# Second layer's heads: exponentials read from the banks by ScalarE, two scalings moved to ScalarE, the mask ahead of the exponential, background pieces moved behind

## The reference, cut to what matters

```python
dmat = jnp.where(order, b[..., :, None] - b[..., None, :] + ig[..., None, :], -jnp.inf)
m_t = jnp.maximum(inter, jnp.max(dmat, axis=-1))
s = jnp.einsum('bhtd,bhsd->bhts', q, k) * jnp.exp(dmat - m_t[..., None])
...
h = num / jnp.maximum(jnp.abs(den), jnp.exp(-m_t))[..., None]
...
h = (h_f + flip(h_b)) if emit else None
...
y = jax.nn.sigmoid(o.astype(f32)).reshape(B, T, M_HEADS, M_DV) * h
y = _rmsnorm(y, hn.reshape(M_HEADS, M_DV)).reshape(B, T, M_V).astype(z.dtype)
return (y * jax.nn.silu(z)) @ w_out
```

## Time and profile before

| | |
|---|---|
| median of three runs | 2987.8 us (2987.46 to 2990.23) |
| profiled execution, its own time | 2990.57 us |
| its span in the profile | 2988.8 us |
| granted TensorE clock, share of full speed | 0.996 |
| busy: PE, DVE, ACT, POOL | 98%, 70%, 39%, 3% of the span |
| heads of the second layer | from about 593 to 1327 us, some 101 us a head |

### The profile page before, as it was taken

One profiled execution on the slowest core, in us unless ns is written; L12 is line 12 of the kernel. 1 busy time (PEld: TensorE's weight loads), 2 busy tenths in 40 slices (PEclk: granted clock), 3 DMA queues, 4 the chain that ended last, 5 costly groups with the idle time before them and its releaser, 6 DMA issues.

```text
span 2988.8 us, 43582 instructions
## 1 busy us (share of the span) xinstructions
PE 2932.5 (98%) x17098; PEld 2353.5 (79%) x17098; DVE 2090.1 (70%) x3957; ACT 1178.0 (39%) x2056; POOL 103.5 (3%) x188
## 2 busy tenths in 40 slices
PE   8999999999999999999999999999999999999999
PEld 7777778888888888878888888888888888885346
DVE  4576876788888776677666886677675678765455
ACT  4322323322332232242245555455444445543344
POOL 0000000000000000000000000000010120000000
PEclk9999999999999999999999999999999999999999
DMA  9777784354555455538636774645576443487997
GB/s 366 281 266 286 273 282 149 127 169 148 190 168 177 162 183 169 179 128 275 235 117 206 258 241 142 197 148 180 195 236 218 141 164 128 152 274 259 403 404 314
DMA packets 193197, 641.69 MB, mean 215 GB/s; under 512 B 21488, under 2 KB 36192, under 8 KB 192992
## 3 DMA queue, kind: packets, MB, share of 16 engines
q1 hardware_dynamic: 132080, 423.44, 40.6%
q10 hardware_dynamic: 58032, 207.12, 20.3%
q0 software_dynamic: 2880, 8.35, 0.9%
HBM read 624.15 MB, written 12.58 MB: 213 GB/s over the span
## 4 chain that ended last, share of the span: by engine, by line
PE 87%; DVE 7%; ACT 3%; DMA 2%; issue 1%; SPq 0%; DVEq 0%; ACTq 0%; POOL 0%; POOLq 0%
PE PS L506 15%; PE PS L502 11%; PE PS L504 9%; PE PS L505 9%; PE PS L635 7%; PE PS L637 7%; PE PS L636 7%; PE PS L1061 2%; PE PS L798 2%; PE PS L1472 2%; DMA AR<-e_w 1%; DVE WL L2389 1%; PE PS L1441 1%; PE PS L1428 1%; PE PS L1122 1%
## 5 line engine op out<-in xcount | busy, mean ns | idle before, releaser
L2389 DVE TENSOR_TENSOR WL<-WR,WH 128x1024 fp32r<-128x1024 f32 (+1 forms) x566 | 682.4, 1211 | 401.7 <-ACT WH L1574 400.5
L506 PE MATMUL PS<-HT,WL 128*128 128x256 f32 (+1 forms) x2928 | 951.5, 325 | 0.0
L1574 ACT ACTIVATE WH<-WR 128x1024 fp32r<-128x1024 f32 (+1 forms) x566 | 587.1, 1044 | 873.1 <-PE PS L506 486.7
L506 PEld LDWEIGHTS PS<-HT,WL 128*128 128x128 f32 x2928 | 552.1, 189 | 47.6
L502 PE MATMUL PS<-HT,WH 128*128 128x512 f32 x1584 | 566.0, 401 | 9.2 <-DVE WL L2389 6.1
L504 PE MATMUL PS<-HT,WH 128*128 128x512 f32 (+1 forms) x1344 | 518.4, 386 | 5.4 <-DVE HT L2369 2.4
L505 PE MATMUL PS<-HT,WH 128*128 128x512 f32 (+1 forms) x1344 | 507.9, 378 | 0.0
L635 PE MATMUL PS<-WH,HT 128*128 128x512 f32 x1016 | 402.7, 396 | 3.5 <-DVE HT L2369 2.5
L637 PE MATMUL PS<-WH,HT 128*128 128x512 f32 x1016 | 396.8, 391 | 0.0
L636 PE MATMUL PS<-WL,HT 128*128 128x512 f32 x1016 | 396.2, 390 | 0.0
L502 PEld LDWEIGHTS PS<-HT,WH 128*128 128x128 f32 x1584 | 297.4, 188 | 90.2 <-issue 13.1
(11 more groups left out here) (472 smaller groups left out, 3319.1 us busy)
## 6 DMA issues: line engine op xcount, KB each, us to landing
WR<-ada_w SPq DMA_DIRECT2D x264, 512.0 KB, 4.6
AR<-e_w SPq DMA_DIRECT2D x88, 512.0 KB, 10.0
E_RING<-e_w SPq DMA_DIRECT2D x80, 512.0 KB, 10.2
WR<-m_vo ACTq DMA_DIRECT2D x64, 512.0 KB, 4.6
WR<-a_qz ACTq DMA_DIRECT2D x64, 512.0 KB, 4.8
WR<-n_m SPq DMA_DIRECT2D x64, 512.0 KB, 4.3
AR<-ada_p ACTq DMA_DIRECT2D x56, 512.0 KB, 6.3
AR<-ada_p SPq DMA_DIRECT2D x48, 512.0 KB, 8.0
```

Of the source, the lines that this page charges most:

```text
L506: return e.matmul(ps[:, 0:b - a], wl, HH_[:, c, a:b], start=False, stop=c == last)
L1574: e.activation(part_of(WH, s), place_of(plan["slot"][p])[:, 0:width(s)], ACT.Copy, scale=1.0).then_inc(*L.up(hi_done, ("hi", s)))
L2389: e.tensor_tensor(part_of(WL, s), place_of(plan["slot"][plan["split"][s]])[:, 0:width(s)], part_of(WH, s).bitcast(F32), ALU.subtract).then ...
```

## The change

Per head:

- VectorE's `ts` (add and clamp) is gone. ScalarE adds the column term itself from the bank, as the bias of the activation: for the diagonal 128x128 blocks with Identity (8 instructions, `pt`), for the whole blocks of `M_REST` straight with Exp (7 instructions). GpSimd masks the diagonal blocks before the exponential, with -3e38, and ScalarE takes their exponential last (8 instructions).
- VectorE multiplies by S only where there is a weight (`M_BLOCKS`): 9 instructions in place of 8, 2560 columns in place of 3072.
- The scaling of the d = 0 results into `M_HH` is done by ScalarE (4 Copy instructions, event `pvx`), and so is the scaling by the inverse root (4, `yn`). VectorE's reciprocals have names now (`pvs`, `yi`) on which ScalarE waits.
- `bg(2)` behind k goes; in `along_vo` the calls at q = 2 and q = 5 take two pieces in place of one, for heads 1 to 7.

```diff
--- before.py
+++ after.py
+    M_BLOCKS = {(0, 0): [(0, 512)], (0, 1): [(0, 128), (256, 512)], (1, 0): [(128, 512)], (1, 1): [(0, 512)],
+                (2, 0): [(256, 512)], (2, 1): [(256, 384)], (3, 0): [(384, 512)], (3, 1): [(256, 512)]}
+    M_REST = {(0, 0): [(128, 512)], (0, 1): [(256, 512)], (1, 0): [(256, 512)], (1, 1): [(0, 128), (256, 512)],
+              (2, 0): [(384, 512)], (2, 1): [], (3, 0): [], (3, 1): [(256, 384)]}
...
@@ scalar_program, mlstm
+            w.wait_ge(L.at("columns"))
             for h in range(8):
+                if h:
+                    w.wait_ge(L.at(("p_used", h - 1)))
+                for d in range(2):
+                    ps, free = place[("cb", h, d)], ("free", ("cb", h, d))
+                    w.wait_ge(L.at(("full", ("cb", h, d))))
+                    for k in range(4):
+                        t = slice(128 * k, 128 * k + 128)
+                        e.activation(M_P[d][:, m_at(k, t.start, t.stop)], ps[:, t], ACT.Identity,
+                                     bias=M_ACOL[:, k, 32 * d + h:32 * d + h + 1], scale=1.0).then_inc(
+                            *L.up(act_done, ("pt", h, k, d), free))
+                    for k in range(4):
+                        for a, b in M_REST[k, d]:
+                            e.activation(M_P[d][:, m_at(k, a, b)], ps[:, a:b], ACT.Exp,
+                                         bias=M_ACOL[:, k, 32 * d + h:32 * d + h + 1], scale=1.0).then_inc(
+                                *L.up(act_done, ("pe", h, k, d), free))
                 for k in range(4):
-                    n = 512 if k < 2 else 256
                     for d in range(2):
-                        p = M_P[d][:, M_PC[k]:M_PC[k] + n]
-                        w.wait_ge(L.at(("pt", h, k, d)))
+                        p = M_P[d][:, m_at(k, 128 * k, 128 * k + 128)]
+                        w.wait_ge(L.at(("pa", h, k, d)))
                         e.activation(p, p, ACT.Exp, scale=1.0).then_inc(*L.up(act_done, ("pe", h, k, d)))
...
+                if h:
+                    w.wait_ge(L.at(("hh_used", h - 1)))
+                for tb in range(4):
+                    w.wait_ge(L.at(("pvs", h, tb, 0)))
+                    e.activation(M_HH[:, tb, :], place[("pv", h, tb, 0)][:, 0:256], ACT.Copy,
+                                 scale=M_ST[2 * tb % 4][:, 0:1]).then_inc(
+                        *L.up(act_done, ("pvx", h, tb), ("free", ("pv", h, tb, 0))))
...
+                w.wait_ge(L.at(("yi", h)))
+                for tb in range(4):
+                    e.activation(M_HH[:, tb, :], M_HH[:, tb, :], ACT.Copy, scale=s[:, 8 + tb:9 + tb]).then_inc(
+                        *L.up(act_done, ("yn", h, tb)))
                 if h < 7:
                     vo(h + 1)
...
@@ vector_program, mlstm
                 for q in range(first, 8):
                     cut_to(plan[("vo", h)][0] + q + NP)
-                    bg(1)
+                    bg(2 if q in (2, 5) and h else 1)
...
             for h in range(8):
-                w.wait_ge(L.at(*(("full", ("cb", h, d)) for d in range(2))))
-                if h:
-                    w.wait_ge(L.at(("p_used", h - 1)))
                 for k in range(4):
                     c0 = 0 if k < 2 else 256
                     for d in range(2):
-                        p = M_P[d][:, M_PC[k]:M_PC[k] + 512 - c0]
-                        ts(p, place[("cb", h, d)][:, c0:512], M_ACOL[:, k, 32 * d + h:32 * d + h + 1], 0.0,
-                           ALU.add, ALU.min, ("pt", h, k, d), *([("free", ("cb", h, d))] if k == 3 else []))
...
-                        w.wait_ge(L.at(("pa", h, k, d), ("full", ("S", h, k))))
-                        tt(p, p, place[("S", h, k)][:, 0:512 - c0], ALU.mult, ("p", h, k, d), ("free", ("S", h, k)))
+                        w.wait_ge(L.at(("pe", h, k, d), ("full", ("S", h, k))))
+                        for a, b in M_BLOCKS[k, d]:
+                            p = M_P[d][:, m_at(k, a, b)]
+                            tt(p, p, place[("S", h, k)][:, a - c0:b - c0], ALU.mult, ("p", h, k, d), ("free", ("S", h, k)))
...
                     elif k == 3 and h < 7:
                         along(("k", h + 1))
-                        bg(2)
...
-                        recip(s, s)
-                        w.wait_ge(L.last(dve_done))
-                        if d == 0:
-                            scaled(M_HH[:, tb, :], ps[:, 0:256], s, ALU.mult, ("free", ("pv", h, tb, d)))
-                        else:
+                        recip(s, s, ("pvs", h, tb, d))
+                        if d:
+                            w.wait_ge(L.last(dve_done), L.at(("pvx", h, tb)))
                             stt(M_HH[:, tb, :], ps[:, 0:256], s, M_HH[:, tb, :], ALU.mult, ALU.add,
...
-                recip(s[:, 8:12], s[:, 8:12])
-                w.wait_ge(L.last(dve_done))
-                for tb in range(4):
-                    scaled(M_HH[:, tb, :], M_HH[:, tb, :], s[:, 8 + tb:9 + tb], ALU.mult, ("yn", h, tb))
+                recip(s[:, 8:12], s[:, 8:12], ("yi", h))
...
@@ gpsimd_program, mlstm
-                        w.wait_ge(L.at(("pe", h, k, d)))
-                        e.affine_select(out=pd, in_=pd, compare_op=ALU.is_ge, fill=0.0, base=0,
+                        w.wait_ge(L.at(("pt", h, k, d)))
+                        e.affine_select(out=pd, in_=pd, compare_op=ALU.is_ge, fill=-3e38, base=0,
```

More of the change, by code:

```diff
@@ L198, in _program, with m_at @@
     M_PC = [0, 512, 1024, 1280]
+    M_BLOCKS = {(0, 0): [(0, 512)], (0, 1): [(0, 128), (256, 512)], (1, 0): [(128, 512)], (1, 1): [(0, 512)],
+                (2, 0): [(256, 512)], (2, 1): [(256, 384)], (3, 0): [(384, 512)], (3, 1): [(256, 512)]}
+    M_REST = {(0, 0): [(128, 512)], (0, 1): [(256, 512)], (1, 0): [(256, 512)], (1, 1): [(0, 128), (256, 512)],
+              (2, 0): [(384, 512)], (2, 1): [], (3, 0): [], (3, 1): [(256, 384)]}
+    def m_at(k, a, b):
+        at = M_PC[k] - (0 if k < 2 else 256)
+        return slice(at + a, at + b)
     M_KEYS = {0: ([0], [0, 1]), 1: ([0, 1], [1]), 2: ([0, 1, 2], [0, 1, 2, 3]), 3: ([0, 1, 2, 3], [0, 1, 3])}
@@ L2911, in mlstm @@
             w.wait_ge(L.at(("full", ("gt",))))
-            copy(SML[:, 0:320], place[("gt",)][:, 0:320], ("free", ("gt",)))
+            copy(SML[:, 0:320], place[("gt",)][:, 0:320], "columns", ("free", ("gt",)))
             w.wait_ge(L.last(dve_done))
             for h in range(8):
-                w.wait_ge(L.at(*(("full", ("cb", h, d)) for d in range(2))))
-                if h:
-                    w.wait_ge(L.at(("p_used", h - 1)))
                 for k in range(4):
@@ L2938, in mlstm @@
                         along(("k", h + 1))
-                        bg(2)
-                if h:
-                    w.wait_ge(L.at(("hh_used", h - 1)))
                 for tb in range(4):
@@ L2945, in mlstm @@
                         s = M_ST[(2 * tb + d) % 4][:, 0:1]
-                        den = ps[:, 256:257]
                         w.wait_ge(L.at(("full", ("pv", h, tb, d))))
-                        stt(s, den, -1.0, M_ECOL[:, tb, 32 * d + h:32 * d + h + 1], ALU.mult, ALU.max)
+                        stt(s, ps[:, 256:257], -1.0, M_ECOL[:, tb, 32 * d + h:32 * d + h + 1], ALU.mult, ALU.max)
                         w.wait_ge(L.last(dve_done))
-                        tt(s, den, s, ALU.max)
+                        tt(s, ps[:, 256:257], s, ALU.max)
                         w.wait_ge(L.last(dve_done))
-                        recip(s, s)
-                        w.wait_ge(L.last(dve_done))
-                        if d == 0:
-                            scaled(M_HH[:, tb, :], ps[:, 0:256], s, ALU.mult, ("free", ("pv", h, tb, d)))
-                        else:
+                        recip(s, s, ("pvs", h, tb, d))
+                        if d:
+                            w.wait_ge(L.last(dve_done), L.at(("pvx", h, tb)))
                             stt(M_HH[:, tb, :], ps[:, 0:256], s, M_HH[:, tb, :], ALU.mult, ALU.add,
@@ L3835, in mlstm @@
             for h in range(8):
[L3836 to L3839, removed]
+                for d in range(2):
+                    for k in range(4):
+                        pd = M_P[d][:, m_at(k, 128 * k, 128 * k + 128)]
                         sg = 1 if d == 0 else -1
-                        w.wait_ge(L.at(("pe", h, k, d)))
-                        e.affine_select(out=pd, in_=pd, compare_op=ALU.is_ge, fill=0.0, base=0,
+                        w.wait_ge(L.at(("pt", h, k, d)))
+                        e.affine_select(out=pd, in_=pd, compare_op=ALU.is_ge, fill=-3e38, base=0,
                                         pattern=[[sg, 128]], channel_multiplier=-sg).then_inc(
```

## The result

The changed kernel takes **2994.35 us** (median of 14 runs, 2990.78 to 3003.14), the kernel before, measured again beside it, 2987.71. The ratio is **1.0025, 95% interval 1.0018 to 1.0032**: slower, by 5.4 to 9.6 us. That lies inside the range of 2985 to 2998 and just above the narrower one of 2988 to 2994. The profiled execution took 2997.0, with a span of 2995.2.

The account below looks back on a forecast made before the run. TensorE, busy for 98% of the span, was taken as the bound, so only its gaps could be won. -4.25 at pv and +8.4 at S gave +4.2 on the median 2987.8: 2992 us, range 2985 to 2998.

Parts of the forecast that it names:

- narrower one of 2988 to 2994: Likeliest case: a stop of 1.1 to 2.6 at each of four places, 0 to +6 us; chance 0.50.
- The gap at pv: TensorE's wait for VectorE at pv, heads 0 to 4: would vanish, 5 x 0.85 = 4.25 us won.
- The scaling for d = 0 and the exponentials on ScalarE: New ScalarE work per head: pv banks freed in time, exponentials done before the next low half is needed; cost 0.
- The scaling by the root: On ScalarE, ahead of the split of vo's piece 2: 0.5 us left of 2.0 in seven heads, no stop.
- the loss at S: First S of heads 1 to 4: TensorE stops 2.1 us for late VectorE each time, 8.4 us.
- The pieces in vo: Ten pieces through two places in vo(1) to vo(4): VectorE late, next head's first S stops 2.1, four times, 8.4 us.
- the refill for which I had reckoned a stop of 0.2: Loads of ada_w in vo: a refill of 4.4 us instead of 5.11 gives -3.4 us in all.
- the sum, -4.25 + 8.4: Whole kernel: gain at pv plus stops at the first S of four heads, +4.2 us.
- within 0.2%: Total time not distinguishable from the kernel before, 0.2% being about 6 us; chance 0.67.
- slower: Total time slower than the kernel before by over 0.2%, about 6 us; chance 0.31.
- clearly slower: Rival at S: refills from about 5.25 on, four stops sum to over 10.2, loss passes 6 us; chance 0.26.

Follow-up runs that it names:

- the three kernels that win it: Changed kernel with pieces around k's last split, 2982.37 us; with one behind it, one extra in vo, 2983.17; kernel before with pieces around that split, 2983.01.
- the kernel with the pieces put back: Changed kernel, but background pieces as before: two behind the last split of k, one at each place in along_vo; 2987.1 us, ratio to before 0.9998.
- two profiles: The changed kernel profiled at first (median 2994.35 us) and once more, unchanged (2996.05 us, ratio 1.0026).
- Short loads: Changed kernel with loads of the ada_w pieces used in heads 0 to 4 cut to 128 of 1024 columns; 2981.5 us, ratio 0.9982.
- the pair of kernels with the fixed lateness: Kernel with pieces around k's last split, plus four idle VectorE products in heads 0 to 3: 3000.51 us; with eleven extra cb matmuls too: 2997.78.

## Why the prediction was right, and where it was not

*The gap at pv.* Right: 8.85 without a stop in heads 0 to 4. Its worth of 4.25 agrees with the three kernels that win it and nothing else is lost in (-0.15 to -0.17%, 4.5 to 5.1 us).

*The scaling for d = 0 and the exponentials on ScalarE, priced at 0.* Right: the kernel with the pieces put back shows both at no cost. The split behind the block starts at 690.53, which is V + 51.0; I had V + 52.1 (692.6) as its bound.

*The scaling by the root.* The split and the low half came where they were forecast (V + 9.3 for V + 9.2), and TensorE does not stop at piece 2. But it is the dearest edit: with it alone undone, the time is that of before or a little less. The prediction had this only as the later start of the pieces (V + 10.33), and didn't say that without it most of the loss at S would be gone.

*The pieces in vo.* Right in mechanism and place, and near in size: VectorE at the transposes at V + 46.4 for V + 46.5, waits of 9.15 and 9.9 us in two profiles for 8.4. Short loads take it all away. Single heads were off, 0.45 to 3.36 for a forecast of 2.1 each: I worked with one refill where each execution draws its own. The agreement of V + 46.4 to a tenth is partly luck: I let four refills of 5.11 in one of the places add up, 3.5 us of waiting, but the three loads waited for belong to both places, with 0.68 + 1.12 + 0.98 = 2.8 us of waiting, and VectorE's other work took the rest longer. The median landing was 4.4, near the refill for which I had reckoned a stop of 0.2: the slow ones among the ten loads made VectorE late, not the middle one.

*The step that failed* is the sum, -4.25 + 8.4. It took a stop to cost its own length. Behind most long stops TensorE went on at half clock and lost 6.8 us more in one profile and 5.1 in the other; the pair of kernels with the fixed lateness shows that it is TensorE's standing still that brings this, not VectorE's lateness (half clock behind three of four stops of 3.44, behind none of four of 0.9, one profile of each). With the gain at 4.25 to 5.1, the first profile gives 9.15 + 6.8 less that, +10.9 to +11.7, and the second 9.9 + 5.1, +9.9 to +10.7. The first two traces bear this out where the heads are: at the transposes that begin head 7 the changed kernel stands 1300.94 - 1289.07 = 11.9 behind; its span ends only 6.4 behind. The two profiled executions themselves stood 9.3 and 10.9 above the median of before, 2.7 and 2.9 above their own. How the typical execution divides its 6.6 or 8.0 between waits and clock is not settled, and half clock also comes elsewhere in the kernel, in other places from run to run (in the profiled execution of before at 1517, 1957 and 2165, in that of the changed kernel at none of the three).

*The chances.* I held "within 0.2%" (0.67) likelier than "slower" (0.31), and it came out slower, by 0.25%. The rival "clearly slower" came closest in its size, but by another mechanism than its own: it wanted refills from 5.25 on, and those waited for in head 1 were 5.06 in the mean.

## What to carry to other kernels

Moving work off VectorE won nothing that can be measured by itself (2987.1 with the pieces put back), and the use made of the freed time here, ten loads through two places, was dearer than the gap it closed; put the background work where the engine already waits for another one. A stop of a saturated TensorE can cost more than its length: at this first S nine of eleven stops of 1.94 us and more cost another 1.5 to 2.7 us each. The start of a chain of refills counts as much as its length.

## What was not expected of the hardware

In all these profiles together, 18 waits of 0.38 to 1.76 us at the first S of a head were followed by a clock of 1.0 each time, and of 11 waits of 1.94 to 3.44 us nine were followed by half clock; the same wait of 3.44 did both in one execution. Where the clock fell, the stretch from S to the next transposes grew from 98.8 us to 100.3 or 100.4, or to between 101.2 and 101.5, and to nothing else. Matmuls without use, in the same place, kept the clock up in four heads of four.

The length of one stop doesn't decide it alone. In the kernel before, further on, three matmuls stand between a wait of 1.42 us and this one of 1.49, both shorter than stops that were harmless at S, and the clock behind them is at 0.5:

```profile
1956.62 0.39 PE L835 MATMUL PS<-WH,HT 128*128 128x256 f32 x1 [1.49 <-POOL HT L3807]
...
1957.20:1960.40 3.20, 3.20 (x17) 0.50 0.43 148
```

At 507 to 510 us two waits of 0.71 and 1.68, again with three matmuls between, are followed by 0.50 as well, and so are those of 0.70 and 1.69 in the changed kernel. So the 1.76 us at S are no bound for other places.
